# A two-layer decoder trunk on one core: the S5 stage rebuilt

## What is computed

```python
A_bar = jnp.exp(A * dt)                                  # 128 groups x 64 complex states
bu = jnp.einsum('bsgc,gpc->bsgp', u.astype(jnp.complex64), B_bar)
_, states = lax.associative_scan(combine, (a, bu), axis=1)   # state_t = A_bar*state_(t-1) + bu_t
y = jnp.einsum('bsgp,gcp->bsgc', states, C_mat).real.reshape(B, S, D)
y = y + d_skip.astype(f32) * h.astype(f32)
z = jax.nn.gelu(y).astype(h.dtype)
val, gate = jnp.split(z @ w_glu, 2, axis=-1)
return val * jax.nn.sigmoid(gate)
```

## Time and profile before

| | |
|---|---|
| median of 3 runs | 2462.67 us (2458.52 to 2462.84) |
| the profiled execution | 2458.5 us, of it 2456.7 us from first to last instruction |
| TensorE matmul busy | 2323.5 us (95%) |
| TensorE weight load busy | 1912.6 us (78%) |
| VectorE busy | 1452.3 us (59%) |
| ScalarE busy | 1030.9 us (42%) |
| GpSimd busy | 220.3 us (9%) |
| HBM | 194 GB/s over the span |
| mean granted TensorE clock | 0.976 of full speed |

### The profile page before, as it was taken

One profiled execution on the slowest core, in us unless ns is written; L12 is line 12 of the kernel. 1 busy time (PEld: TensorE's weight loads), 2 busy tenths in 40 slices (PEclk: granted clock), 3 DMA queues, 4 the chain that ended last, 5 costly groups with the idle time before them and its releaser, 6 DMA issues.

```text
span 2456.7 us, 32749 instructions
## 1 busy us (share of the span) xinstructions
PE 2323.5 (95%) x10950; PEld 1912.6 (78%) x10950; DVE 1452.3 (59%) x1918; ACT 1030.9 (42%) x1127; POOL 220.3 (9%) x327
## 2 busy tenths in 40 slices
PE   8999898999999999999947599989999999999996
PEld 6888687888888888888835588778888888888885
DVE  5545757566667775567737655465445444444455
ACT  4443534444444334443333154344544433344432
POOL 0000058401111111001300000000000000000000
PEclk9999999999999999999968799999999999999998
DMA  7555164768787667757784165555555555555553
GB/s 238 184 185 163 63 226 138 247 226 267 255 256 260 229 221 239 234 198 250 234 198 150 52 202 188 174 189 193 190 189 188 192 190 192 193 188 188 189 192 116
DMA packets 135856, 483.02 MB, mean 197 GB/s; under 512 B 16496, under 2 KB 18032, under 8 KB 134608
## 3 DMA queue, kind: packets, MB, share of 16 engines
q1 hardware_dynamic: 120432, 429.44, 53.5%
q0 software_dynamic: 14048, 50.80, 6.6%
q10 hardware_dynamic: 1280, 1.48, 0.2%
HBM read 457.80 MB, written 19.14 MB: 194 GB/s over the span
## 4 chain that ended last, share of the span: by engine, by line
PE 90%; DVE 5%; DMA 2%; issue 1%; ACT 1%; DVEq 0%; SPq 0%; ACTq 0%
PE ps L352 28%; PE ps L354 28%; PE ps L353 28%; PE ps L368 1%; PE ps L650 1%; PE ps L611 1%; DVE w_lo L994 1%; DMA h_quarter<-res 1%; DMA raw<-in_w_in 1%; DVE gated L1571 1%; DVE gated L1569 1%; DMA raw<-in_w_glu 1%; DVE res L1224 0%; ACT w_hi L711 0%; PE ps L625 0%
## 5 line engine op out<-in xcount | busy, mean ns | idle before, releaser
L994 DVE TENSOR_TENSOR w_lo<-raw,w_hi 128x1024 fp32r<-128x1024 f32 x775 | 950.4, 1229 | 850.1 <-ACT w_hi L711 847.3
L711 ACT ACTIVATE w_hi<-raw 128x1024 fp32r<-128x1024 f32 x775 | 820.4, 1060 | 1173.7 <-PE ps L354 1135.3
L352 PE MATMUL ps<-w_hi,x_hi 128*128 128x512 f32 x2304 | 905.7, 393 | 18.5 <-DVE x_lo L1002 15.1
L354 PE MATMUL ps<-w_hi,x_lo 128*128 128x512 f32 x2304 | 899.4, 390 | 0.0
L353 PE MATMUL ps<-w_lo,x_hi 128*128 128x512 f32 x2304 | 899.0, 390 | 0.0
L352 PEld LDWEIGHTS ps<-w_hi,x_hi 128*128 128x128 f32 x2304 | 434.2, 188 | 109.3 <-DVE x_lo L1002 17.0
L354 PEld LDWEIGHTS ps<-w_hi,x_lo 128*128 128x128 f32 x2304 | 433.9, 188 | 91.4
L353 PEld LDWEIGHTS ps<-w_lo,x_hi 128*128 128x128 f32 x2304 | 434.3, 189 | 88.7
L352 PE MATMUL ps<-w_hi,hid_hi 128*128 128x512 f32 x704 | 275.2, 391 | 0.0
L353 PE MATMUL ps<-w_lo,hid_hi 128*128 128x512 f32 x704 | 274.1, 389 | 0.0
L354 PE MATMUL ps<-w_hi,hid_lo 128*128 128x512 f32 x704 | 274.0, 389 | 0.0
(11 more groups left out here) (210 smaller groups left out, 1350.4 us busy)
## 6 DMA issues: line engine op xcount, KB each, us to landing
raw<-in_w_inA SPq DMA_DIRECT2D x192, 512.0 KB, 4.3
raw<-in_w_inB SPq DMA_DIRECT2D x160, 512.0 KB, 4.3
raw<-in_w_outA SPq DMA_DIRECT2D x96, 512.0 KB, 4.3
raw<-in_w_outB SPq DMA_DIRECT2D x80, 512.0 KB, 4.2
raw<-in_w_in SPq DMA_DIRECT2D x64, 512.0 KB, 4.1
raw<-in_w_gate SPq DMA_DIRECT2D x64, 512.0 KB, 4.3
raw<-in_w_glu SPq DMA_DIRECT2D x64, 512.0 KB, 4.3
raw<-in_w_out SPq DMA_DIRECT2D x32, 512.0 KB, 4.2
```

Source lines behind the costliest of these rows:

```text
L352: pe.matmul(o, hi[:, kt + k, cols], WH[:, s, k, 0:width], start=(kt + k == 0), stop=False)
L354: last = pe.matmul(o, lo[:, kt + k, cols], WH[:, s, k, 0:width], start=False, stop=(kt + k == depth - 1))
L711: act.activation(WH[:, s, :, 0:width], RAW[:, s, :, 0:width], ACT.Copy).then_inc(hi_ready, 1)
L994: dve.tensor_tensor(WL[:, s, :, 0:width], RAW[:, s, :, 0:width], WH[:, s, :, 0:width].bitcast(F32), ALU.subtract).then_inc(lo_ready, 1)
```

## The change

The S5 stage between `outB0` and `glu` is rebuilt.

- **Rows scaled in place.** `norm_quarter(1, ..)` goes. DVE and ACT only centre and scale the rows of the residual (4 instructions of 512 columns each, `hat_dve`, `hat_act`). TensorE turns them feature by feature (32 transposes, which also put the tokens in the order of the slots); gain and bias of the LayerNorm are per-partition numbers then and are applied as the turned rows leave PSUM (`UT`, 8 instructions on each of DVE and ACT). The residual itself gets gain and bias later, inside `glu` (`norm_late`, 8 instructions of 1024 columns on DVE). The move through DMAs (L304), its re-ordering (L914) and L599, L924 go.
- **A move on TensorE**: 32 products of a 32x32 piece of the identity with 512 columns bring the four tokens of a slot onto the partitions of a pair (`U4`).
- **Tables held in TensorE**: for each of 16 rows 8 products, table (128x128) stationary, 64 slots of `U4` streamed. The result has states on partitions, so that one ACT copy per row of 512 writes `ST`; L932, L625, L1552 and L937 go.
- **Two-level scan**: for each row DVE first joins slots in twos (`join`, 3 instructions), then chains the 31 joined values (`chain_op`, 30 steps, two halves of 8 rows interleaved), then fills in the other slots (`grow`, 3 instructions for each row); ACT copies the chain back (`even_states`).
- **Feature-major read-out**: the short response (`KTAB` held, 256 products with 32 rows and 32 columns, 64 to 256 streamed) starts when the first half's chain has done 15 steps; then, behind `grow`, 32 products for each row (128 rows by 32 columns held, 64 slots of `ST` streamed). GELU writes feature-major, so L663 goes. The assembling of `KK` by POOL goes.
- **Fillers**: products of the identity with itself whose result nobody reads: 6 and 10 at the start, 3 in each of six steps of the attention, 18 at the first chunk of either `gate`, 36 behind `outB0`.
- **Loads**: input tables 2 to 9 come during `outB0`, one for every fourth chunk, six more behind the first four `glu` chunks; LayerNorm's `gb` for the second norm is loaded once the input products are done. Chunks 4 to 7 of `glu` wait for `grow` and `even_states`, since the chain lies in the raw ring.

Core of the diff (lines as in the change, parts left out):

```diff
@@ layout @@
-        H4 = at("h_steps", [SLOTS, PAIRS, SUB, PW], 112)
-        ST = at("states", [P, SLOTS, 2, PAIRS], 112)
-        U4 = at("u", [P, PAIRS, SLOTS], 144)
+        ST = at("states", [P, KT, 2, 4, SLOTS], 112)
+        CH = [at(f"chain{h}", [P, SLOTS // 2, PAIRS], 8 - 8 * h) for h in range(2)]
+        U4 = at("u_by_pair", [P, 4, KT, SLOTS], 96)
+        UT = at("u", [P, KT, SUB, SLOTS], 144)
+        slot_kb = [160, 164, 48, 64, 52, 68, 56, 72, 60, 76, 168, 172, 176, 180]
@@ SP @@
+            def out_with_tables():
+                nb, per, c0, _ = PHASES["outB0"]
+                for j in range(nb * per):
+                    load(t["w_outB0"], j, c0 + j, 0, None, WB)
+                    if j == RING:
+                        sp.wait_ge(w_used, c0)
+                        sp.wait_ge(e_stored[0], 16 * 11)
+                        sp.wait_ge(e_stored[1], 16 * 5)
+                    if j >= 8 and j % 4 == 0:
+                        input_table(j // 4)
...
-                for q4 in range(4):
-                    quarter_normed(sp, 4 + q4 + 1)
...
-                    for q in range(TT):
-                        sp.dma_start(HQ[q4 % 2][32 * q:32 * q + 32, :, :], RES[:, q, cols]).then_inc(h4_in[q4 % 2], 16)
...
+                for row in (0, 1, 10, 11, 12, 13):
+                    input_table(row)
...
+                for row in range(2, 14):
+                    sp.wait_ge(e_done, row + 1)
+                    output_table(row)
...
+                for h in range(2):
+                    sp.wait_ge(grown, 24 * (h + 1))
+                    sp.wait_ge(even_out, 8 * (h + 1))
+                    glu_chunks(RING + h, RING + 1 + 3 * h)
@@ TensorE @@
+            def fill(out, count):
+                for _ in range(count):
+                    pe.matmul(out, ID[:], ID[:], start=True, stop=True)
...
+                            if j == 0:
+                                fill(Y[:, 1, 0:P], 18)
                             pe.wait_ge(turned, g0 + j + 1)
...
-                    for a in range(4):
-                        last = pe.matmul(PS[0:SLOTS, 2 * (tile % 2) + a // 2, TOK * (a % 2):TOK * (a % 2 + 1)],
-                                         U4[:, 4 * tile + a, :], TS[tile % 6][:, a].rearrange("p c n -> p (c n)"),
...
-                            last = pe.transpose(PS[:, 4 + tile % 4, o:o + SLOTS], EM[tile % 2][:, a, ri, :],
...
-            for pair in range(PAIRS):
-                pe.matmul(bank_of(pair), U4[:, pair, :], KK[:, pair, :], start=(pair % 4 == 0), stop=False,
...
+            pe.wait_ge(k_out, 2 * 7)
+            fill(Y[:, 0, 0:P], 36)
...
+            for row in range(KT):
+                if row % 8 < 2:
+                    pe.wait_ge(hat_dve, 2 * (row // 8) + row % 8 + 1)
+                    pe.wait_ge(hat_act, 2 * (row // 8) + row % 8 + 1)
+                for q in range(TT):
+                    o = PS[:, row // 2, TOK * (row % 2):TOK * (row % 2 + 1)].rearrange("p (s q n) -> p q n s", s=SUB, q=TT)[:, q]
+                    last = pe.matmul(o, RES[:, q, P * tile_of(row):P * (tile_of(row) + 1)],
+                                     ID[:].rearrange("p (n s) -> p n s", s=SUB), start=True, stop=True, is_transpose=True)
...
+            for h in range(2):
+                pe.wait_ge(u_dve, 4 * (h + 1))
+                pe.wait_ge(u_act, 4 * (h + 1))
+                for s in range(SUB):
                     for a in range(4):
+                        rows = slice(PW * a, PW * (a + 1))
+                        last = pe.matmul(PS[PW * s:PW * (s + 1), 4 * h + a, :], ID[rows, rows], UT[rows, 8 * h:8 * h + 8, s, :],
                                          start=True, stop=True)
...
+            for row in range(KT):
+                pe.wait_ge(ts_in[row % 14], 16 if row < 14 else 32)
...
+                for ri in range(2):
                     for a in range(4):
+                        o = (4 * ri + a) * SLOTS
+                        last = pe.matmul(PS[:, row % 8, o:o + SLOTS], TS[row % 14][:, a, ri, :], U4[:, a, row, :], start=True, stop=True)
+                last.then_inc(e_done, 1)
...
+            pe.wait_ge(e_out, KT)
+            pe.wait_ge(scan[0], 3 * 15)
+            for row in range(KT):
+                for lag in range(SUB):
+                    for a in range(4):
+                        rows = slice(PW * a, PW * (a + 1))
+                        pe.matmul(outputs(row, a, lag, SUB), KTAB[rows, tile_of(row), lag, :],
+                                  UT[rows, row, 0:SUB - lag, :].rearrange("p s n -> p (s n)"),
+                                  start=(row % 2 == 0 and lag == 0), stop=False, skip_group_check=True)
+            for row in range(KT):
...
+                pe.wait_ge(grown, 6 * (row // 2) + 5 + row % 2)
+                pe.wait_ge(even_out, row + 1)
+                for s in range(SUB):
                     for ri in range(2):
+                        for a in range(4):
+                            last = pe.matmul(outputs(row, a, s, s + 1), TS[row % 14][:, a, ri, PW * s:PW * (s + 1)],
+                                             ST[:, row, ri, a, :], start=False, stop=(ri == 1), skip_group_check=True)
                 last.then_inc(y_done, 1)
@@ ScalarE @@
+            for n_ in (0, 2, 1, 3):
+                part = RES[:, 1, WB * n_:WB * (n_ + 1)]
+                act.activation(part, part, ACT.Identity, bias=SC[:, 23:24], scale=SC[:, 17:18]).then_inc(hat_act, 1)
...
+            for row in range(KT):
+                act.wait_ge(e_done, row + 1)
+                act.activation(ST[:, row].rearrange("p c a n -> p (c a n)"), PS[:, row % 8, :], ACT.Copy).then_inc(e_out, 1)
...
+                act.activation(ST[:, row].rearrange("p c a n -> p (c a) n")[:, :, 2:SLOTS:2],
+                               CH[row // 8][:, 1:SLOTS // 2, first:first + 8].rearrange("p m x -> p x m"), ACT.Copy).then_inc(even_out, 1)
@@ VectorE @@
-            for q4 in range(4):
-                norm_quarter(1, q4)
...
+            for n_ in (0, 2, 1, 3):
+                part = RES[:, 0, WB * n_:WB * (n_ + 1)]
+                dve.tensor_scalar(part, part, MV[:, 0, 0:1], SC[:, 16:17], ALU.subtract, ALU.mult).then_inc(hat_dve, 1)
...
+            MID = SLOTS // 2 - 1
...
+            def join(row, n_):
...
+                if n_ == 0:
+                    dve.wait_ge(e_out, row + 1)
+                    ins = product(row, slots_of(row, 1))
+                elif n_ == 1:
+                    ins = total(row)
+                else:
+                    ins = dve.tensor_tensor(chain_of(row, 1), wide[row % 2][:, :, 0], slots_of(row, 2), ALU.add)
+            def grow(row, n_):
...
+                if n_ == 0:
+                    ins = product(row, chain_of(row, 1))
+                elif n_ == 1:
+                    ins = total(row)
+                else:
+                    ins = dve.tensor_tensor(slots_of(row, 3), slots_of(row, 3), wide[row % 2][:, :, 0], ALU.add)
...
+            for k in range(1, MID):
+                for n_ in range(3):
+                    for h in range(2):
+                        chain_op(h, n_, k)
@@ GpSimd @@
-            pool.memset(KK[:], 0.0).then_inc(kk_zero, 1)
...
-                    pool.dma_start(KK[PW * s:PW * (s + 1), r::4, PW * s:P],
...
+            pool.wait_ge(e_done, KT)
+            load_gb(1)
```

More of the change, by code:

```diff
@@ L381, in _ @@
             turn_x(1)
+            fill(Y[:, 1, 0:P], 10)
             _, per, c0, b0 = PHASES["win"]
@@ new lines, in even_states @@
+            def even_states(row):
+                if row % 8 == 0:
+                    act.wait_ge(scan[row // 8], 3 * (SLOTS // 2 - 2))
+                first = 8 * (row % 8)
+                act.activation(ST[:, row].rearrange("p c a n -> p (c a) n")[:, :, 2:SLOTS:2],
+                               CH[row // 8][:, 1:SLOTS // 2, first:first + 8].rearrange("p m x -> p x m"), ACT.Copy).then_inc(even_out, 1)
+            for row in range(8):
+                even_states(row)
+            for row in range(8, KT):
+                even_states(row)
@@ L1564, in scan_op, with chain_op @@
+            dve.wait_ge(lo_ready, PHASES["glu"][2] + RING)
+            for row in range(0, KT, 2):
+                for n_ in range(3):
+                    join(row, n_)
+                    join(row + 1, n_)
+            dve.wait_ge(square, 7)
+            dve.wait_ge(joined, 3 * KT)
+            def chain_op(h, n_, k):
+                done = 3 * (k - 1) + n_
                 if done > 0:
-                    dve.wait_ge(scan[h], lin(done, 3 * per, i))
-                m = slice(half * h, half * (h + 1))
@@ L1567, in scan_op @@
-                x, y = (ST[:, bass.ds(lin(k + d, per, i), 1)].rearrange("p a c n -> p (a c) n")[:, :, m] for d in (1, 2))
+                    dve.wait_ge(scan[h], done)
+                prod = SW[:, h, 0:2, :].rearrange("p c n -> p (c n)")
+                part = SW[:, h, 2, :]
+                x, y = CH[h][:, k, :], CH[h][:, k + 1, :]
                 if n_ == 0:
```

(31 more changed lines are left out.)

338 lines of the change are left out of this document (145 added, 193 removed).

## The result

The changed kernel takes **2393.7 us** (median of 4 runs, 2393.34 to 2396.09) against 2461.82 (4 runs of before on the same chip, 2458.52 to 2462.84): ratio 0.9728, 95% interval [0.9716, 0.9741], 68 us less. The forecast was 2401, with 2384 to 2436.

A forecast was written before the change was run, and what follows sets the result against it. Projections bound most of the kernel, a chain of small steps the 177.4 us S5 stage; 59.7 us from `glu` starting earlier plus 2 from the gates gave 2396.8 profiled, 2401 for the median, range 2384 to 2436.

The forecast's parts named there:

- the late `glu` chunk: End of `outB0`: a chunk delayed beside POOL's Toeplitz DMAs held up L1302; without them it starts 3.8 us earlier.
- rival D: Behind `outB0`: fillers don't hold the clock, 2 to 3 us lost and none of the gates' 2: 2406; chance 0.1.
- Input products: S5 stage: 256 instructions paced by weight loads at 0.11 us each, 28.2 us in all, ending at 1284.
- Transposes: Behind the fillers in the S5 stage: 32 at 0.085 us each take 2.7 us, to 1248.7.
- The move: S5 stage: 64 instructions of 512 columns, four overlapping, take 7.1 us, to 1256; bounds 1.8 to 28.5.
- The chain: DVE's scan: 30 steps of 6 instructions at 0.195 us each take 35.2 us, to 1323, against 87.8 before.
- Grow: DVE behind the chain: 1.8 us per row with a strided read of 1.16, 28.8 us in all, to 1352.
- The read-out: End of the stage: 1024 instructions at 0.027 us, 28 us, just under `grow`; PE ends two rows behind, at 1355.5.
- rival B: Read-out bound by its many instructions: at 0.06 us each 61 us, to 1388, kernel 2434; chance 0.16.
- The response's cover: Short response starts 17.6 us into the chain, takes 17.8 plus 2; 21 us of cover, so costs nothing.
- Rival A: Short response doesn't overlap, its row tiles writing one PSUM bank: 71 us alone, kernel 2452; chance 0.12.
- Gates: First chunks of `gate0` and `gate1`: 18 fillers fill the gap and keep the clock up, together 2 us gained.

The follow-up runs named there:

- the turned order: Changed kernel with the loops of the move and the short response turned inside out, so that neighbouring pieces share their 32 rows: 2466.6 us (one run).

## Why the prediction was right, and where it wasn't

**Right.** Every removed wait went where the prediction put it; no rival's time came. But that the time came out so near is partly luck: the steps up to `grow` were 13.7 us too dear in the forecast and the read-out 8.4 too cheap, and the two offset each other. L1302 began right behind PE, and the late `glu` chunk was its cause (the run with late Toeplitz DMAs). Fillers held the clock (rival D fell: 1.00 in the window 1240 to 1250). Input products went at 28.77 / 256 = 0.112 against 0.11, by the row with the same weights. The response took 20.4 us against 17.8 + 2. `join` ran under the products, the chain began 3.1 us behind the last of them (forecast 4). `norm_late` and the moved loads show no stall in `outB0` or `glu`.

**Mis-sized, harmless.** Transposes 0.11 each instead of 0.085. The move 2.6 us in all (2.3 in its two bursts) instead of 7.1: sixteen pieces overlap, not four. The trace is even under the lower end of what the Trainium skill (TensorE: Matmul & The Clock Gate) gave, 2.7.

**The chain.** The step "50 instructions fill 10 us, so 0.20 each (0.195 without the loop)" failed. The pitch was that of a hardware loop's instructions, and the change writes them out: 0.158 each, 28.5 us for the 180 instead of 35.2. I had taken the loop's price for its overhead at each turn; the run of before written out shows that it sits in each step.

**Grow.** The groups of DVE by form, changed kernel, from 1254 to 1345 (busy, mean ns of one):

```profile
L1591 DVE TENSOR_TENSOR gated<-a_bar,chain 128x496 f32<-128x496 f32 x16 | 16.1, 1045 | 0.1
...
L1591 DVE TENSOR_TENSOR gated<-a_bar,states 128x496 f32<-128x496 f32 x16 | 10.7, 671 | 5.9 <-ACT states L931 5.9
```

I took 1.16 us for the strided read of `chain` and 0.66 for the read of `states`; they are 1.05 and 0.67. The strided cost is there, but smaller than the copies of the earlier trace rows have it, and a row goes every 1.62 us instead of 1.8: 26 us instead of 28.8.

**The read-out: a right number for a wrong reason.** 0.027 us for each piece was taken from L554, as the pace of four column groups. The array's pace is 0.014, and what the kernel gets is 31.8 / 1024 = 0.031, the pace at which 256-instruction blocks arrive beside its other transfers. That is rival B in kind, bound by its many instructions, at half of B's price, though B argued from the loads and not from the arrival of the code. The sentence "so PE ends two rows behind it" failed for it: the read-out never waited for DVE, and `glu` began 12 us behind `grow`, not 3 to 4; 8.4 of the 13.7 us by which the steps up to `grow` were faster went there. Hence a stage only 5.3 us too high.

**From the stage to the time.** With 2 us for the gates the profiled execution was forecast at 2396.8 and took 2393.3. The step from there to the median, 4.2 us, was the offset of the one profiled execution of before; the changed kernel's lay 0.4 under its median. So 7.3 us between 2401 and 2393.7 are 3.5 of the kernel and 3.8 of that offset.

**The response's cover.** I wrote that beyond its cover every us counts, and gave it 21 us. It began 14.3 us into the chain and not 17.6, and the chain ended 28.5 behind its start: 14.2 us of cover and 3.3 of `grow`'s first pair. It ran 2.9 us past that pair (1320.8 against 1317.9). Without the wait on `scan[0]` the read-out starts 3.0 us earlier and the stage is 3.0 shorter, which is this.

**Rival A** was priced at 71 us for pieces one by one. By the Trainium skill (TensorEngine Tiling (Array Packing), on PSUM pressure) row tiles of one bank can't go at once; the response's pieces do, at 0.040. With most of the overlap gone the response took 96.8 us in a real run, and the kernel then is at 2466.6. So the danger was real, but it lay in the order of two loops, which the prediction didn't look at, and in a clock that stayed at 0.50, where A had only 2 us for a cold start.

**Rival D.** The 0.88 that it reads as a share of the window is the window's mean clock; the 1282.4 that it works with does follow from that.

**Gates.** Forecast 2 us for both; `gate0` shows 1.3 (12.0 to 10.7 between its turns), and 2.5 against no fillers. No timing resolves it.

**Open.** What a filler in the attention costs; why a block takes 3.5 us to come (and up to 5.9 beside `glu`'s loads, a gap of 3.9 behind a burst of 1.99); what the turned order costs at the full clock; and whether a looped read-out would escape the fetch, which wasn't tried.

## What to carry to other kernels

Count instructions as you count columns: a burst of matmuls shorter than 0.028 us each with their loads was paced here by the arrival of its code, so fewer and longer pieces beat a perfectly packed array, and such a burst should start as early as its first data allow. Order small pieces so that no two neighbours have both rows and columns of the array in common, and look at the granted clock beside it; the same 512 instructions took 20 or 97 us, part of it the clock's. Before a scan on VectorE is restructured, write its loop out: 13 us (8 to 16 by the interval), a fifth of what the whole change brought, were to be had from that alone.

## What the runs showed of the hardware that I had not expected

- PE stalls every 127 matmuls with their loads (about 256 instructions, eight 16-KB transfers for 2048), one block each 3.50 us alone; after 15 to 20 us of standing still it has 295 to 331 pairs at hand.
- Sixteen 32x32 pieces of 512 columns overlap almost fully: 32 instructions in 1.14 us, 0.036 each, where one takes 0.45 alone by the earlier trace rows.
- Overlap needs another row group *or* another column group than the piece before: different columns alone are enough (the move in the turned order, 1.14). With neither, the response took 0.189 for each at a granted clock of 0.50.
- The clock, down after 17 us of waiting, came back within 10 us of the response in one order (0.88 from 1305, 1.00 from 1310) and in the other not in 96.8 us of uninterrupted work (0.50 to 1395).
- An instruction of DVE in the loop of before costs 0.195 at a pitch and 0.158 written out, with the same shapes.
- Steps of 256 bytes between elements cost a read of 496 elements 1.05 us instead of 0.67 (steps of 8 bytes).
